# A transformer layer with a mixture of experts: the experts' rows turned before they are normalized, and expert 1 requested at its own block count

## The reference

```python
x = x + gt1 * y
h = rmsnorm(x, p['g_norm2']) * (1.0 + sc2) + sh2
x = x + gt2 * moe(h, p)

logits = (xt @ p['w_router']) + p['b_router']
topv, topi = lax.top_k(logits, TOP_K)
wts = jax.nn.softmax(topv, axis=-1)
...                                   # tokens sorted by expert, in blocks
gu = xb @ p['w_gu'][e] + p['b_gu'][e]
act = (up + 1.0) * gate * jax.nn.sigmoid(SWIGLU_ALPHA * gate)
yb = (act @ p['w_down'][e] + p['b_down'][e]) * w[:, None]
```

## Time and profile before

| | us |
|---|---|
| median of 3 runs | 1567.43 (1558.92 to 1570.28) |
| profiled execution | 1574.77 |
| its span | 1573.2 |
| PE busy | 1338.3 (85%) |
| DVE busy | 681.6 (43%) |
| ACT busy | 204.0 (13%) |
| POOL busy | 191.5 (12%) |
| DMA, mean over the span | 322 GB/s |

### The profile page before, as it was taken

How to read it: one execution, slowest core, us unless ns; L and a number is a source line. 1 busy time by engine, 2 the same in 40 slices (tenths; PEclk the granted TensorE clock), 3 DMA queues, 4 the chain that set the end, 5 groups by cost and what they waited for, 6 DMA issues and landing times.

```text
span 1573.2 us, 40569 instructions
## 1 busy us (share of the span) xinstructions
PE 1338.3 (85%) x16239; PEld 746.3 (47%) x16240; DVE 681.6 (43%) x1471; ACT 204.0 (13%) x463; POOL 191.5 (12%) x249
## 2 busy tenths in 40 slices
PE   5997989999998789979999696876949978869693
PEld 2455656367676545534555353433424434435352
DVE  2434656453635444534544343522523525325344
ACT  1124532311110210000000000000000000000001
POOL 2021310000000111111111111111111111120200
PEclk9999999988899899989999898987979979889797
DMA  9744992950093379699999999999999987996961
GB/s 353 264 170 137 349 397 105 345 193 1 12 324 151 134 302 417 276 424 422 425 425 425 429 428 427 429 429 428 415 428 418 415 346 332 425 428 286 414 271 63
DMA packets 63251, 505.83 MB, mean 322 GB/s; under 512 B 6528, under 2 KB 6648, under 8 KB 35332
## 3 DMA queue, kind: packets, MB, share of 16 engines
q1 hardware_dynamic: 55396, 480.98, 74.7%
q0 software_dynamic: 7808, 24.24, 4.6%
HBM read 500.09 MB, written 5.11 MB: 321 GB/s over the span
## 4 chain that ended last, share of the span: by engine, by line
PE 63%; DMA 15%; DVE 7%; issue 7%; POOL 3%; ACT 2%; SPq 2%; POOLq 0%; ACTq 0%; DVEq 0%
PE psum L558 59%; DMA ring<-in_w_gu 13%; POOL ring L2310 2%; DMA ring<-in_w_ada 2%; PE psum L727 2%; ACT region L1919 1%; DVE region L1837 1%; DVE region L1349 1%; SPq L2362 1%; DVE region L1194 1%; PE psum L759 0%; POOL region L2288 0%; DVE region L1817 0%; SPq L2387 0%; SPq L2388 0%
## 5 line engine op out<-in xcount | busy, mean ns | idle before, releaser
L558 PE MATMUL psum<-ring,region 128*32 128x256 f32 (+3 forms) x11328 | 724.6, 391 | 138.0 <-DMA ring<-in_w_gu 133.5
L558 PEld LDWEIGHTS psum<-ring,region 128*32 128x32 f32 (+2 forms) x11328 | 388.3, 114 | 443.2 <-DMA ring<-in_w_gu 154.5
L558 PE MATMUL psum<-region 32*128 32x320 f32 (+10 forms) x2714 | 252.9, 422 | 8.2 <-ACT region L1919 1.9
L2310 POOL COPY ring<-region 128x1024 f32<-128x1024 f32 x124 | 123.7, 1041 | 869.7 <-PE psum L558 869.7
L1817 DVE TENSOR_TENSOR region<-region,psum 128x1280 f32<-128x1280 f32 x110 | 161.3, 1467 | 119.4 <-PE psum L558 119.4
L1700 DVE TENSOR_SCALAR region<-psum,region 128x320 f32<-128x320 f32 x55 | 30.3, 551 | 346.9 <-PE psum L558 346.9
L1919 ACT ACTIVATE region<-psum 128x256 f32<-128x256 f32 (+7 forms) x164 | 72.6, 448 | 793.9 <-PE psum L558 697.6
L558 PE MATMUL psum<-region,ring 128*128 128x320 f32 (+1 forms) x640 | 174.0, 428 | 1.6 <-DVE region L1604 1.4
L558 PEld LDWEIGHTS psum<-region 128*32 128x32 f32 (+5 forms) x2714 | 102.8, 138 | 133.4 <-issue 91.4
L558 PEld LDWEIGHTS psum<-region,ring 128*128 128x128 f32 x640 | 119.6, 197 | 50.7 <-issue 8.4
L1686 DVE TENSOR_SCALAR region<-region 128x32 f32<-128x32 f32 x165 | 29.3, 238 | 85.6 <-issue 85.6
(11 more groups left out here) (335 smaller groups left out, 779.6 us busy)
## 6 DMA issues: line engine op xcount, KB each, us to landing
ring<-in_w_gu SPq DMA_DIRECT2D x128, 2048.0 KB, 12.1
ring<-in_w_down SPq DMA_DIRECT2D x33, 2048.0 KB, 10.5
region<-in_w_down SPq DMA_DIRECT2D x31, 2048.0 KB, 9.7
ring<-in_w_ada SPq DMA_DIRECT2D x12, 2048.0 KB, 14.2
ring<-in_w_in SPq DMA_DIRECT2D x11, 2048.0 KB, 20.2
ring<-in_cache_k SPq DMA_DIRECT2D x64, 256.0 KB, 5.4
ring<-in_cache_v POOLq DMA_DIRECT2D x64, 256.0 KB, 5.7
ring<-in_w_out SPq DMA_DIRECT2D x2, 2048.0 KB, 21.9
```

What stands on the lines that cost most here:

```text
L558: return pe.matmul(out, lhsT, rhs, start=start, stop=stop, skip_group_check=True)
L2310: pool.tensor_copy(ring[:, moe_slot[n], part], landing[i][:, part])\
```

## The change

Seven things, by the name that they have in the code:

- **Rows turned unnormalized.** `turn_rows` no longer uses transposes of a finished `hT`. For each token tile and half of the features it multiplies `hT` itself (times gain, not yet normalized) by the identity, on top of a product of nine shift rows with `cond_std`, the 0/1 table of conditions times the root. So the bank holds (x gain + root x shift), and ScalarE multiplies by the reciprocal root per token as it copies (`copy_rows_of`, scale `rstd_tok`). GpSimd's eight multiplications and its addition, and ScalarE's eight additions, are gone. The rows of the third tile are turned after `pos`.
- **Shift rows.** `shift_rows`: the nine shifts as rows, at partitions 0, 32, 64 and 96, made by TensorE in banks 6 and 7 between the last `upb` product and the output projection, copied by ScalarE after `bd_cleared`.
- **Logits unscaled.** The shift logits times `cond_std` are added in the bank of the raw logits; ScalarE copies it, three products turn it, and the top-four search sees logits times the root. Only the differences to the best are multiplied by `rstd_tok`.
- **Table load.** ScalarE runs a Sqrt on one word ahead of the wait for `ss2`.
- **Expert 1 at its own count.** VectorE writes expert 0's block count as soon as it is known (`first_blocks`); SP reads that and asks for expert 1 without waiting for `tables`. Its loop starts at expert 2.
- **Weights later.** `hot4w` and `wts` move from before `cum` to before `list`.
- **Rounds later.** The addition that makes `pos` from `eq` moves behind `tables`.

```diff
@@ shift rows and router, PE
             pe.wait_ge(hm_ready, 1)
             up("upb", hmT)
+            for half in range(2):
+                out = claim(pe, (6, 7), "shift_rows", half)
+                for i in range(4):
+                    for g in range(0, P, 32):
+                        last = mm(out[g:g + 9, P * i:P * i + P], modT[:, 24 + 4 * half + i, :], ident, True, True)
+                last.then_inc(full_sem("shift_rows", half), 1)
...
-            router_part(1).then_inc(full_sem("part_logits"), 1)
+            router_part(1)
...
+            def turn_rows(j, half):
+                t0, n = TILES[j]
+                pe.wait_ge(*drained("shift_rows", half))
+                out = claim(pe, (2, 3, 4, 5, 6), "h2", j, half)
+                rows = slice(64 * (j % 2) + 32 * half, 64 * (j % 2) + 32 * half + 9)
+                mm(out[0:n, :], cond_std[rows, t0:t0 + n], shift_rows[rows, 512 * half:512 * half + 512], True, False)
+                for i in range(4):
+                    last = mm(out[0:n, P * i:P * i + P], hT[:, 4 * half + i, t0:t0 + n], ident, False, i == 3)
+                last.then_inc(full_sem("h2", j, half), 1)
+
+            pe.wait_ge(cond_ready, 1)
+            turn_rows(0, 0)
             pe.wait_ge(*drained("shift_logits"))
+            mm(bank("part_logits")[0:NE, 0:NT], shift_logits[0:9, :], cond_std[0:9, :], False, True)\
+                .then_inc(full_sem("part_logits"), 1)
+            turn_rows(0, 1)
             pe.wait_ge(*drained("part_logits"))
             out = claim(pe, (1,), "logit")
             for j, (t0, n) in enumerate(TILES):
-                rows = out[0:n, NE * j:NE * j + NE]
-                mm(rows, part_logits[:, t0:t0 + n], const("expert_hot")[:, 0:NE], True, False)
-                last = mm(rows, const("cond_hot", 9)[:, t0:t0 + n], shift_logits[0:9, :], False, True)
+                last = mm(out[0:n, NE * j:NE * j + NE], part_logits[:, t0:t0 + n], const("expert_hot")[:, 0:NE],
+                          True, True)
             last.then_inc(full_sem("logit"), 1)
-            pe.wait_ge(h_shifted, 2 * KT)
-            pe.wait_ge(h2_ready, 1)
+            pe.wait_ge(rstd2_ready, 1)
+            out = claim(pe, (0,), "rstd_tok")
             for j, (t0, n) in enumerate(TILES):
-                for half in range(2):
-                    out = claim(pe, (2, 3, 4, 5, 6, 7), "h2", j, half)
-                    for i in range(4):
-                        last = pe.transpose(out[0:n, P * i:P * i + P], hT[:, 4 * half + i, t0:t0 + n], ident)
-                    last.then_inc(full_sem("h2", j, half), 1)
+                last = mm(out[0:n, j:j + 1], rstd[0:1, t0:t0 + n], ones[0:1, 0:1], True, True)
+            last.then_inc(full_sem("rstd_tok"), 1)
+            for half in range(2):
+                turn_rows(1, half)
...
             last.then_inc(full_sem("pos"), 1)
+            for half in range(2):
+                turn_rows(2, half)
@@ DVE
+            dve.tensor_tensor(cond_std, const("cond_hot"), rstd[:], ALU.mult).then_inc(cond_ready, 1)
+            dve.wait_ge(*own(cond_ready))
             dve.reciprocal(rstd[:], rstd[:]).then_inc(rstd2_ready, 1)
             dve.wait_ge(*own(rstd2_ready))
-            dve.wait_ge(*full("part_logits"))
-            dve.tensor_tensor(part_logits, bank("part_logits")[:, 0:NT], rstd[:], ALU.mult)\
-                .then_inc(free_sem("part_logits"), 1)
...
+            dve.wait_ge(*drained("rstd_tok"))
+            dve.tensor_tensor(ew, ew, over(rstd_tok, 2, 4), ALU.mult).then_inc(top_diff, 1)
...
+            dve.tensor_copy(ints[0:1, AT_BLOCKS:AT_BLOCKS + 1], plan[0:1, 0:1]).then_inc(first_blocks, 1)
@@ ACT
+            for half in range(2):
+                act.wait_ge(bd_cleared, 1)
+                act.wait_ge(*full("shift_rows", half))
+                copy(shift_rows[:, 512 * half:512 * half + 512], bank("shift_rows", half))\
+                    .then_inc(free_sem("shift_rows", half), 1)
+                act.wait_ge(*drained("shift_rows", half))
             act.wait_ge(eps_set, 1)
+            act.activation(pool_act, EPS_COL[0:1, :], ACT.Sqrt).then_inc(act_step, 1)
...
-            shift_prompt(1, 24)
...
+                    act.activation(h2_tok[0:n, j, 512 * half:512 * half + 512], bank("h2", j, half)[0:n, :],
+                                   ACT.Identity, scale=rstd_tok[0:n, j:j + 1])\
+                        .then_inc(free_sem("h2", j, half), 1)
@@ POOL
-            for k in range(KT):
-                pool.tensor_tensor(hT[:, k, :], hT[:, k, :], rstd[:], ALU.mult).then_inc(h_scaled, 1)
-            pool.wait_ge(h_scaled, 2 * KT)
...
@@ SP
             sp.wait_ge(*full("h2", 2, 1))
             fill_landing(0, slice(1, 2))
...
+            sp.wait_ge(first_blocks, 1)
+            expert_weights(slice(1, 2), sp.value_load(ints[0:1, AT_BLOCKS:AT_BLOCKS + 1], min_val=1,
+                                                      max_val=MAX_BLOCKS))
             sp.wait_ge(tables, 1)
-            with sp.Fori(1, NE - 1) as e:
+            filled_behind(1, bass.ds(sp.value_load(ints[0:1, AT_ORDER + 2:AT_ORDER + 3], min_val=0, max_val=NE - 1), 1))
+            with sp.Fori(2, NE - 1) as e:
...
```

More of the change, by code:

```diff
@@ L275, in build @@
         selwT = E.take(NT)
+        shift_rows = Area(E.at).take(D)
+        assert E.at + D <= fin_at + KT * NT + 2 * FF
         E.at = max(E.at, fin_at + KT * NT + 2 * FF)
@@ L282, in build @@
         part_logits = fin_junk[:, 0:NT]
+        cond_std = fin_add[:, 0:NT]
+        rstd_tok = E.take(3)
         split_rows = Area(E.at).take(2 * NT)
@@ L399, in build @@
         rstd2_ready = sem("rstd2_ready")
+        cond_ready = sem("cond_ready")
+        first_blocks = sem("first_blocks")
         top_diff = sem("top_diff")
@@ L1056, in _ @@
             SIDE = (B_Y, B_SUM, B_SUM + 1, B_SUM + 2, B_SUM + 3)
+            POS = 7
             pe.wait_ge(routed, 1)
-            out = claim(pe, SIDE, "pos")
+            out = claim(pe, (POS,), "pos")
             before = const("before")
@@ L1766, in _ @@
             dve.tensor_copy(ints[0:1, AT_ORDER:AT_ORDER + NE], bank("cum")[0:1, 2 * NE:3 * NE])
-            dve.tensor_copy(ints[0:1, AT_BLOCKS:AT_BLOCKS + NE], bank("cum")[0:1, NE:2 * NE])\
+            dve.tensor_copy(ints[0:1, AT_BLOCKS + 1:AT_BLOCKS + NE], bank("cum")[0:1, NE + 1:2 * NE])\
                 .then_inc(free_sem("cum"), 1)
@@ L1776, in _ @@
             dve.wait_ge(*own(begun_ready))
-            rounds = pos.rearrange("p j (r e) -> p j r e", r=ROUNDS)
-            step(dve.tensor_tensor(rounds, over(eq, 2, ROUNDS),
-                                   over(const("round_start").rearrange("p (r e) -> p r e", r=ROUNDS), 1, 3),
-                                   ALU.add))
+            step(dve.tensor_tensor(hot4w, hot4, over(ew, 3, NE), ALU.mult))
+            dve.tensor_reduce(wts, hot4w.rearrange("p j s e -> p j e s"), AX, ALU.add).then_inc(weights_ready, 1)
+            dve.wait_ge(*own(weights_ready))
             dve.wait_ge(*full("list"))
@@ L1795, in _ @@
             dve.wait_ge(*own(tables))
+            rounds = pos.rearrange("p j (r e) -> p j r e", r=ROUNDS)
+            step(dve.tensor_tensor(rounds, over(eq, 2, ROUNDS),
+                                   over(const("round_start").rearrange("p (r e) -> p r e", r=ROUNDS), 1, 3),
+                                   ALU.add))
             def first_weights():
@@ L2158, in _, with copy_rows_of @@
             act.wait_ge(*own(mean_root2))
+            act.wait_ge(*full("part_logits"))
+            copy(part_logits, bank("part_logits")[:, 0:NT]).then_inc(free_sem("part_logits"), 1)
+            act.wait_ge(*drained("part_logits"))
             act.activation(pool_act, EPS_COL[0:1, :], ACT.Exp).then_inc(free_sem("ss2"), 1)
-            shift_prompt(1, 24)
+            act.wait_ge(*drained("ss2"))
+            act.wait_ge(*full("rstd_tok"))
+            for j, (t0, n) in enumerate(TILES):
+                last = copy(rstd_tok[0:n, j:j + 1], bank("rstd_tok")[0:n, j:j + 1])
+            last.then_inc(free_sem("rstd_tok"), 1)
+            act.wait_ge(*drained("rstd_tok"))
+            def copy_rows_of(j):
+                t0, n = TILES[j]
+                for half in range(2):
+                    act.wait_ge(*full("h2", j, half))
+                    act.activation(h2_tok[0:n, j, 512 * half:512 * half + 512], bank("h2", j, half)[0:n, :],
+                                   ACT.Identity, scale=rstd_tok[0:n, j:j + 1])\
+                        .then_inc(free_sem("h2", j, half), 1)
+                    act.wait_ge(*drained("h2", j, half))
+            copy_rows_of(0)
             act.wait_ge(top_diff, 1)
@@ L2163, in _ @@
             act.wait_ge(*own(top_exp))
-            for j, (t0, n) in enumerate(TILES):
-                for half in range(2):
-                    act.wait_ge(*full("h2", j, half))
-                    copy(h2_tok[0:n, j, 512 * half:512 * half + 512], bank("h2", j, half)[0:n, :])\
```

(5 more changed lines are left out.)

30 lines of the change are left out of this document (11 added, 19 removed).

## The result

The changed kernel takes 1588.33 us in the median of 6 runs (1577.0 to 1594.52), the kernel before 1568.86 beside it (6 runs, 1558.92 to 1574.38). The ratio is 1.0121, with a 95% interval of 1.0074 to 1.0169: **slower by 1.2%**, where 1570.5, and with a chance of 0.92 no difference beyond about 1%, had been forecast.

| stretch | before | after | difference |
|---|---|---|---|
| start of the span to the end of clearing `bd_rows` | 491.13 | 487.39 | -3.7 |
| end of the clearing to the last sum of squares | 37.16 | 39.03 | +1.9 |
| last sum of squares to block 1's first product ("D" below) | 46.02 | 58.23 | **+12.2** |
| block 1 to the end | 998.8 | 1002.9 | +4.1 |

A forecast was written before the change was run, and what follows sets the result against it. One line of dependent work up to block 1 was taken to bound the kernel. Output projection +2 and the steps from there to block 1 +1 made +3 on the median 1567.43: 1570.5 us, range 1561 to 1578.

The forecast's parts named there:

- part two: Last sum of squares to the places: rows turned in half tiles of 1.78 us, logits, places and `gather` all earlier.
- Part one: Output projection: tile 1 waits for bank 6, a 5 us gap with 1.2 GHz behind it, +2 (-0.1 to +2.8).
- Logits: Behind the last sum: VectorE sees the logits at 536.1 instead of 537.01, -0.9.
- Places: Behind the routing: places no longer queue behind the transposes, there at 544.0 instead of 548.39, -4.4.
- the clock's term: Third tile's rows: about 2 us idle ahead of `pos` lowers the clock, a good half at 1.2 GHz, +1.7 (0 to +3.6).
- The tables: From `gather` to block 1: `tables` 1.9 to 2.5 us earlier, the moved addition +1.2 ahead of the next `sel`.
- some 7 us earlier than 560.9: SP's queue: the request for expert 1 goes out near 553 to 556, with no gain by itself.
- The second: Rival, chance 0.22: third tile's rows between `pos` and `gather` take 7.1 us at 1.2 GHz; +7, 1574.5.
- The first rival: Chance 0.25: TensorE's clock stays up and the gains stand; at best -1.4, 1566.0.
- parts two and three: Last sum to block 1, through rows, places and tables: -0.7 plus 1.7 for the clock, together +1.0.
- The third: Rival, chance 0.08: block 1 was waiting for its weights and gains at most 2.2 us; +0.8, 1568.
- The fourth: Rival, chance 0.03: in the turned rows a product costs four transposes instead of two, 0.44 us; 1574.1.

The follow-up runs named there:

- e6: Kernel before plus only the early request for expert 1, SP's loop starting at expert 2: 1574.66 us, ratio 1.0031 to the kernel before.
- e1: Changed kernel with the six shift products reading all 128 rows instead of nine: 1579.01 us, ratio 1.0059 to the kernel before.
- e10: e7 run again unchanged, beside another run on the same chip: 1562.58 us, ratio 0.9958 to the kernel before.
- e5: Kernel before, profiled once more with no edit, for the spread between executions: 1571.04 us.
- e4: Changed kernel with bank 6 claimed behind the products of feature tile 1, not ahead: 1582.97 us, ratio 1.0095 to the kernel before.
- e7: Changed kernel with 128-row shift products, bank 6 claimed behind tile 1, addition ahead of the list, SP's requests as before: 1566.01 us, ratio 0.9971.
- e8: e7 with the early request for expert 1 kept: 1570.1 us, ratio 0.9999 to the kernel before.
- e3: Changed kernel without the shift products and with transposes instead of identity products: 1577.16 us, ratio 1.0047 to the kernel before.
- e2: Changed kernel with the six shift products left out, identity products kept: 1575.2 us, ratio 1.0016 to the kernel before.

## Why the prediction was wrong

**The step that failed** is TensorE's clock in part two: a half tile was priced at 1.78 us at 2.4 GHz, and "a good half" of the third tile alone at 1.2 GHz, +1.7. The reason given was that the clock falls after an idle time, read from the gaps of the earlier trace rows; that it could fall under the rows themselves had no term. The idle time of 2 us that was to bring it down did not come: the clock fell in the middle of work at 533.5, and the rows of the second tile reached past the routing. Nor does an idle time alone decide: e6 has the 2.89 us of the earlier trace rows with no fall behind them. What the fall cost, by the same steps in the changed kernel and in e1:

| step | after | e1 | difference |
|---|---|---|---|
| last sum to the second tile's rows | 10.53 | 8.69 | +1.84 |
| second tile's rows to `pos` | 7.88 | 3.89 | +3.99 |
| `pos` and its small products | 2.43 | 1.49 | +0.94 |
| third tile's rows to `gather` | 9.01 | 5.03 | +3.98 |
| `gather` to block 0 | 4.73 | 3.43 | +1.30 |
| block 0 to block 1 | 23.65 | 22.78 | +0.87 |

The sum, 12.92 where +1.7 (at most +3.6) was forecast, is more than the 12.21 by which D grew over before; what the change would have gained there without the clock, 0.71, is hardly more than the 0.45 between the two executions of before. At 2.4 GHz the price was right: 1.85 measured, 1.78 worked out. Of the 19.5 us between the two medians D has some 12, the lead 2 to 5, and the request some 5, an estimate from single executions and from e6 to e10.

**Part one** was right in mechanism: tile 1 waited for bank 6 to 488.12, 5.04 us ended by ScalarE (5 forecast), and the clock fell behind it. That the lead grew by 1.87 where +2 was forecast is in part luck. It is counted from a lead of 37.16 with a fall of the clock in it; the same stretch takes 35.68 in e5 and 34.23 in e6, and against these the wait cost 3.4 and 4.8. e4 has 34.29 without the wait.

**Logits** -0.9 forecast, +0.75 measured; e1 gives -0.59. **Places** -4.4 forecast, +0.93 measured: that the second tile's rows end ahead of the routing fell with the clock, and `pos` (544.83) had to queue behind them. e1 gives -5.85, so the mechanism stands at full clock. **`gather`** was forecast 0.4 later with the clock's term; it came 8.77 later, in e1 1.99 earlier.

**The tables.** Block 0 to block 1 took 23.65 instead of 21.14. The addition moved behind `tables` was priced right: +1.2 forecast, and putting it back (e7 and e10 against e1) shortens the stretch from 22.78 to 21.5.

**SP.** The request was to go out "some 7 us earlier than 560.9" and to cost nothing; both were wrong. It went out at 564.80, since block 0 read its first unit late (against the last sum, it comes 3.7 us earlier in e6 than in before and 4.5 earlier in e8 than in e7); and it costs some 0.3% (e6 to e10), which no view of the kernel before shows. So the loop did not only move, as the prediction had it.

**The rivals.** The second, slower by the third tile's rows between `pos` and `gather`, had the right place and sign, and the 7.1 us for two half tiles at 1.2 GHz (7.65 measured). Its cause, the order, was not it: e1 keeps the order and has `gather` earlier than before. It missed the second tile's rows, which were slow as well, and gave +7 in all. The first rival's -0.7 to -1.3 for parts two and three is what e1 shows once the rows are 128 (D 0.71 below that of before). The third is not borne out: block 1 waited 3.08 us for TensorE's own list, as before, and in e6 an earlier request left D where it was. The fourth was a price. At 2.4 GHz a product costs 1.6 transposes, not two as worked out: a transpose takes 0.14 us there (e3), where the 0.22 of the earlier trace rows at 1.2 GHz had been halved. The Trainium skill, "TensorE: Matmul & The Clock Gate", section "Terms", has a factor of four for FP32; these 1.6 do not agree. In the range, the two ends were built on a clock that only gaps bring down; the result lies 10 us above the upper one.

## What to carry to other kernels

A price in TensorE time holds at one level of its clock: for a new kind of product, here nine rows of 128, look for a row that shows which level such products were granted, and where there is none, keep a case in the range in which all of them run at 1.2 GHz. Moving work on TensorE into the shadow of another engine is only worth what is left when that work runs at half speed. And where one queue feeds a chain of weights, time at the head of its loop can be on the path at every expert: here 0.11 us came back 11 times.

## What the runs showed of the hardware

- TensorE busy without a gap had its clock granted at 1.2 GHz from 533.5 on, through 21 us of products of nine rows and identity products; the same columns over 128 rows (e1, e7 to e10) had 2.4 GHz, and with identity products alone (e2) it was at 1.2 GHz for 3.4 us of the rows.
- An idle time did not decide by itself. Behind the same 2.9 us ahead of the first sum, the granted clock over the next 8 us was 0.63 in the kernel before and 1.00 in e6, whose code is the same up to there.
- Shorter work ran longer: e3's transposes (0.55 us for four, against 0.89) left an idle time of 2.78 us, and the stretch at 1.2 GHz behind it cost more than they saved (D 44.36 against 41.60).
- SP took 0.11 us longer from the landing request to the next expert's when the loop began at 2 instead of 1, in every one of 11 gaps of all kernels with that loop. The cause was not found.
